# Modulation vectors of a two-layer backbone: silu(c) as the stationary operand in four column tiles

## What is computed

```python
def modulation(cvec, w, b):
    m = jax.nn.silu(cvec) @ w + b
    return [z[:, None, :] for z in jnp.split(m, N_MOD, axis=-1)]

def block(x, mods, nw, fw_in, fw_out, mixer, params, init_state):
    sh1, sc1, g1, sh2, sc2, g2 = mods
    h = rms_norm(x, nw[0]) * (1 + sc1) + sh1
    out, state = mixer(h, init_state, *params)
    x = x + g1 * out
    h = rms_norm(x, nw[1]) * (1 + sc2) + sh2
    x = x + g2 * swiglu(h, fw_in, fw_out)
    return x, state
...
        mods_p = modulation(c_ctx[None, :], mod_w[l], mod_b[l])
        mods_s = modulation(c, mod_w[l], mod_b[l])
```

## Time and profile before

| What | Value |
|---|---|
| Time, median of 3 runs | 3576.94 us (3574.57 to 3578.27) |
| Span of the profiled execution | 3571.6 us |
| TensorE matmul busy | 3069.0 us, 86% of the span |
| TensorE weight loads busy | 2459.5 us, 69% |
| VectorE busy | 1515.4 us, 42% |
| ScalarE busy | 728.8 us, 20% |
| Chain that ended last | TensorE 73%, VectorE 18%, ScalarE 3% |
| Line 377 on that chain | 3% |

### The profile page before, as it was taken

One profiled execution on the slowest core, in us unless ns is written; L12 is line 12 of the kernel. 1 busy time (PEld: TensorE's weight loads), 2 busy tenths in 40 slices (PEclk: granted clock), 3 DMA queues, 4 the chain that ended last, 5 costly groups with the idle time before them and its releaser, 6 DMA issues.

```text
span 3571.6 us, 49794 instructions
## 1 busy us (share of the span) xinstructions
PE 3069.0 (86%) x20104; PEld 2459.5 (69%) x20104; DVE 1515.4 (42%) x2905; ACT 728.8 (20%) x1161; POOL 0.2 (0%) x4
## 2 busy tenths in 40 slices
PE   7799869883999998799989688888887497999897
PEld 6687769763889985588868445555554285888686
DVE  1310655557666562322232336666666513222323
ACT  0321200020111100322221213333333313222211
POOL 0000000000000000000000000000000000000000
PEclk6899556655999977899999889999998698999998
DMA  5122412221000012122212122222222021222121
GB/s 165 41 71 57 118 48 77 75 60 32 5 2 2 2 43 80 42 70 70 70 55 71 37 55 71 72 71 77 73 71 73 7 60 40 71 70 70 56 68 53
DMA packets 404830, 210.10 MB, mean 59 GB/s; under 512 B 13368, under 2 KB 402886, under 8 KB 404550
## 3 DMA queue, kind: packets, MB, share of 16 engines
q1 hardware_dynamic: 345344, 173.36, 16.9%
q10 hardware_dynamic: 59334, 34.66, 3.2%
HBM read 202.32 MB, written 5.67 MB: 58 GB/s over the span
## 4 chain that ended last, share of the span: by engine, by line
PE 73%; DVE 18%; ACT 3%; issue 3%; DVEq 1%; ACTq 1%; DMA 1%
PE bank L250 10%; PE bank L251 9%; PE bank L252 9%; PE bank L253 9%; PE bank L1733 7%; PE bank L377 3%; PE bank L1055 3%; PE bank L230 2%; PE bank L1734 2%; PE bank L443 2%; PE bank L1777 2%; PE bank L1774 2%; PE bank L1107 1%; PE bank L1113 1%; DVE wide_low L270 1%
## 5 line engine op out<-in xcount | busy, mean ns | idle before, releaser
L253 PEld LDWEIGHTS bank<-arena,ring 128*128 128x128 f32 x2816 | 537.3, 191 | 129.0
L253 PE MATMUL bank<-arena,ring 128*128 128x128 f32 x2816 | 545.1, 276 | 0.0
L250 PE MATMUL bank<-h_split,w_split 128*128 128x512 f32 x928 | 450.1, 485 | 65.7 <-DVE w_split L260 65.7
L260 DVE TENSOR_TENSOR w_split<-ring,w_split 128x1024 fp32r<-128x1024 f32 x180 | 214.9, 1201 | 561.3 <-ACT w_split L257 552.4
L1733 PE MATMUL bank<-arena,ring 128*128 128x512 f32 x768 | 410.6, 617 | 2.1 <-ACTq L196 2.1
L251 PE MATMUL bank<-h_split,w_split 128*128 128x512 f32 x928 | 370.2, 399 | 0.0
L252 PE MATMUL bank<-h_split,w_split 128*128 128x512 f32 x928 | 369.3, 398 | 0.0
L257 ACT ACTIVATE w_split<-ring 128x1024 fp32r<-128x1024 f32 x180 | 186.1, 1040 | 729.0 <-PE bank L253 378.4
L250 PE MATMUL bank<-wide_high,w_split 128*128 128x512 f32 x480 | 234.1, 488 | 76.6 <-DVE w_split L260 76.6
L377 PEld LDWEIGHTS bank<-cs_T,ring 128*128 128x128 f32 x1536 | 292.9, 297 | 2.6 <-issue 1.4
L377 PE MATMUL bank<-cs_T,ring 128*128 128x2 f32 x1536 | 288.9, 323 | 2.1 <-ACTq L196 2.1
(11 more groups left out here) (351 smaller groups left out, 4245.2 us busy)
## 6 DMA issues: line engine op xcount, KB each, us to landing
ring<-in_mod_w_dram SPq DMA_DIRECT2D x96, 512.0 KB, 3.7
ring<-in_ffn_w_in_dram SPq DMA_DIRECT2D x88, 512.0 KB, 3.6
ring<-in_od_w_in_dram SPq DMA_DIRECT2D x48, 512.0 KB, 3.8
arena<-cumulative_decays ACTq DMA_DIRECT2D x80, 256.0 KB, 3.5
ring<-in_ffn_w_out_dram SPq DMA_DIRECT2D x32, 512.0 KB, 3.8
ring<-in_ev_w_in_dram SPq DMA_DIRECT2D x30, 512.0 KB, 3.5
ring<-in_od_w_out_dram SPq DMA_DIRECT2D x16, 512.0 KB, 3.8
ring<-in_ffn_w_out_dram SPq DMA_DIRECT2D x16, 384.0 KB, 3.3
```

Of the source, the lines that this page charges most:

```text
L250: E.matmul(o, w_split[:, ws, 0, k, :], high(k), start=st, stop=False)
L253: mm = E.matmul(pair[pr][:, CTX], ring[:, s, k, :], rhs[:, k, CTX], start=st, stop=en)
L260: return V.tensor_tensor(w_split[:, ws, 1, 0:kt], ring[:, s, 0:kt], w_split[:, ws, 0, 0:kt].bitcast(F32), ALU.subtract)
```

## The change

`cs_T` becomes 8 chunks of 32 columns, of which 2 hold data and 30 are zero. It is now the stationary operand, and the weights stream. The class `Mods` works in groups of 8 output tiles (`GT`). A group has two rounds. In a round the four ring slots hold, for 4 of the 8 chunks of features, 256 output columns each: slot s columns 256 s to 256 s + 255. For each chunk, four matmuls write 32 partitions each of one PSUM area of 256 columns, slot s to partitions 32 s to 32 s + 31: four column tiles of TensorE. Over both rounds 32 matmuls accumulate, where there were 64. The last four matmuls of a round count up `unit_done`, so the ring's slots come free at the end of a round. The DMA of a slot takes 4 chunks x 256 columns (runs of 1 KB in memory) instead of 8 x 128 (runs of 512 B), with the same 512 KB.

The result has the two vectors on partitions and outputs along the columns. `copy` (VectorE) brings it to `mod_rows` in SBUF, `turn` (TensorE) transposes its two halves, `bias` (VectorE) adds the bias from PSUM into `mod` and waits for its own end (`mod_made`). Where `stage_mod` and `stage_conv` have two groups, they use two PSUM banks.

The places are these: `stage_mod` two groups; `stage_conv` two groups, all four rounds first and then both turns on TensorE, and on VectorE the copy of group 0 behind the convolutions, the bias of group 0 and the copy of group 1 behind the eighth token shift, the bias of group 1 at the end; the mLSTM head one group, its rounds where units 1, 2 and 3, 4 stood, its turn behind the third chunk of transposes; the mLSTM loop three groups, rounds in iterations 3, 5 and 7 (middle and end), turns in iterations 4, 6 and 8; the other four stages one group each, with rounds in their passes 0 and 1.

Besides, the semaphores of `stage_norm` are shared by all norms, with running counts, the arena is 120 columns smaller, and a memset of `cs_T` stands first on VectorE.

```diff
-    cs_T = sb("cs_T", [P, KD, 2])
+    cs_T = sb("cs_T", [P, KD, 32])
+    mod_rows = sb("mod_rows", [P, 2 * P])
...
+            V.memset(cs_T[:, :, :], 0.0)
...
-    def mod_unit(out, s):
-        for k in range(KD):
-            mm = E.matmul(out, ring[:, s, k, :], cs_T[:, k, :], start=(k == 0), stop=(k == KD - 1))
-        mm.then_inc(unit_done, 1)
...
+        def fetches(self, sp):
+            for g in range(self.ng):
+                t = self.t0 + GT * g
+                w = a["mod_w"][t // 48, :, :].rearrange("(k p) n -> p k n", p=P)
+                for r in range(2):
                     for s in range(4):
+                        c0 = (t % 48) * P + s * 2 * P
+                        sp.wait_ge(unit_done, self.u0 + GT * g + 4 * r + s + 1)
+                        sp.dma_start(ring[:, s, :, :].rearrange("p a b -> p (a b)").rearrange("p (k n) -> p k n", k=4),
+                                     w[:, 4 * r:4 * r + 4, c0:c0 + 2 * P]).then_inc(w_ready[s], 16)
+
+        def products(self, pe, g, r):
+            q = self.u0 // 4 + 2 * g + r
+            for s in range(4):
+                pe.wait_ge(w_ready[s], q * 16 + 16)
+            if r == 0 and g >= len(self.banks):
+                pe.wait_ge(mod_made, self.g0 + g - len(self.banks) + 1)
+            for kk in range(4):
+                k = 4 * r + kk
+                for s in range(4):
+                    w = ring[:, s, :, :].rearrange("p a b -> p (a b)")[:, kk * 2 * P:(kk + 1) * 2 * P]
+                    mm = E.matmul(self.acc(g)[32 * s:32 * s + 32, :], cs_T[:, k, :], w, start=(k == 0), stop=(k == KD - 1))
+                    if kk == 3:
+                        mm.then_inc(unit_done, 1)
+
+        def turn(self, pe, g):
+            pe.wait_ge(mod_copied, self.g0 + g + 1)
+            for h in range(2):
+                mm = E.transpose(self.turned(g)[:, h * P:(h + 1) * P], mod_rows[:, h * P:(h + 1) * P], ident)
+            mm.then_inc(mod_turned, 1)
+
+        def copy(self, dve, g):
+            dve.wait_ge(unit_done, self.u0 + GT * (g + 1) + 4)
+            V.tensor_copy(mod_rows[:, :], self.acc(g)).then_inc(mod_copied, 1)
+
+        def bias(self, dve, g):
+            t = self.t0 + GT * g
+            dve.wait_ge(mod_turned, self.g0 + g + 1)
+            V.tensor_tensor(mod[:, t:t + GT, :].rearrange("p (s h) c -> p s h c", h=2),
+                            self.turned(g).rearrange("p (h s z) -> p s h z", h=2, s=4)[:, :, :, 0:2],
+                            vec[:, V_MODB + t:V_MODB + t + GT].rearrange("p (s h) -> p s h", h=2)
+                            .unsqueeze(3).to_broadcast([P, 4, 2, 2]), ALU.add).then_inc(mod_made, 1)
+            dve.wait_ge(mod_made, self.g0 + g + 1)
...
+            m.copy(dve, 0)
...
+                if k == 7:
+                    m.bias(dve, 0)
+                    m.copy(dve, 1)
+            m.bias(dve, 1)
...
-        return (lambda pe: make(pe, 16)), act, dve, fetches
+        def pe(pe):
+            for g in range(2):
+                for r in range(2):
+                    m.products(pe, g, r)
+            for g in range(2):
+                m.turn(pe, g)
...
-            make_a(pe, 2)
+            ma.products(pe, 0, 0)
...
-            make_a(pe, 2)
+            ma.products(pe, 0, 1)
...
-                make_a(pe, 1 if c < CT else 0)
+                if c == 2:
+                    ma.turn(pe, 0)
...
-                make_b(pe, 1 if n > 2 else 0)
+                if n in (3, 5, 7):
+                    mb.products(pe, (n - 3) // 2, 0)
+                if n in (4, 6, 8):
+                    mb.turn(pe, (n - 4) // 2)
...
-                make_b(pe, 3 if n == 2 else 2 if n > 2 else 0)
+                if n in (3, 5, 7):
+                    mb.products(pe, (n - 3) // 2, 1)
```

More of the change, by code:

```diff
@@ L357, in stage_load @@
         return pe, act, dve
-    MOD0 = 2 * KD
+    GT = 8
     mod_tiles = [0]
[L366 to L371, removed]
-                    for s in range(4):
-                        fetch(sp, s, i + (u0 + a0 - t0) // 4, w[:, :, bass.ds(i * (4 * P) + (a0 - 48 * l + s) * P, P)], KD, P)
@@ L413, in col, with dve @@
+    def stage_mod():
+        m = Mods(2, (4, 5))
+        def pe(pe):
+            m.products(pe, 0, 0)
+            m.products(pe, 0, 1)
+            m.products(pe, 1, 0)
+            m.turn(pe, 0)
+            m.products(pe, 1, 1)
+            m.turn(pe, 1)
+        def dve(dve):
+            for g in range(2):
+                m.copy(dve, g)
+                m.bias(dve, g)
+        return pe, (lambda act: None), dve, m.fetches
     def col(v, n=1):
         return vec[:, v:v + n]
-    def stage_norm(src, dst, kt, scale_at, weight, shift_at, name):
-        sq_s, ss_s, m_s, rt_s, h_s = (sem(f"{name}_{n}") for n in ("squares", "sum", "mean", "root", "scaled"))
+    sq_s, ss_s, m_s, rt_s, h_s = (sem(f"norm_{n}") for n in ("squares", "sum", "mean", "root", "scaled"))
@@ L421, in stage_norm @@
+    norm_tiles, norms = [0], [0]
+    def stage_norm(src, dst, kt, scale_at, weight, shift_at):
+        k0, n0 = norm_tiles[0], norms[0]
+        norm_tiles[0] += kt
+        norms[0] += 1
         sq = dst if kt == KD else take(2, T)
@@ L849, in dve @@
                 dve.sem_inc(st_s, 1)
+                if n in (3, 5, 7):
+                    mb.copy(dve, (n - 3) // 2)
+                if n in (4, 6, 8):
+                    mb.bias(dve, (n - 4) // 2)
                 if n == 1:
@@ L915, in dve @@
                 finish(dve, j)
-            mod_end(dve)
-        return pe, act, dve, fetches
+                if j == 2:
+                    m.copy(dve, 0)
+            m.bias(dve, 0)
+        return pe, act, dve, m.fetches
     def finish_mlstm(ha, vo):
@@ L970, in pe @@
                 mm.then_inc(p_s, 1)
-                make(pe, 2)
+                if j < 2:
+                    m.products(pe, 0, j)
+            m.turn(pe, 0)
         def dve(dve):
```

98 lines of the change are left out of this document (48 added, 50 removed).

## The result

The changed kernel takes 3523.01 us, the kernel before 3575.76: a ratio of 0.9846 (95% interval 0.9832 to 0.986; the quotient of the two medians is 0.9852). The forecast was 25.7 us less, 3551, with a range of 3536 to 3565; the sign was right and the size was not. The profiled execution of the changed kernel takes 3521.53 us, its span is 3519.8 (3571.6 before), so the median lies 3.2 over the span, where the forecast had kept 5.3.

The account below looks back on a forecast made before the run. It took TensorE's 1536 weight loads and matmuls (289 us) as the price, counting where they end a chain of waits. Terms -14.4 +3.2 -13.7 -1.8 +1.5 -0.5 = -25.7: span 3545.9, median 3551 us, range 3536 to 3565.

Parts of the forecast that it names:

- the round (3.6): On TensorE, 16 matmuls of 256 columns in four side-by-side column tiles take 3.6 us at the lower clock.
- the refill in the first stage (8.2): Each later round waits 8.2 us for four 512 KB loads from a standing start; bounds 6.8 and 9.0.
- the head's second round: In the mLSTM head, the second round ends after its refill at 450.3 against 453.02 before: -2.7 us.
- Rivals 1 and 3: Column-tile lanes: 1, overlap only in pairs, round 6.9, total 3607 us, 9%; 3, overlap with loss, round 4.3, 3563, 11%.
- Rival 2: Streaming keeps TensorE's clock at its upper level, so rounds take 1.9 us everywhere: 3539 us; chance 13%.
- Rival 4: Refills are far slower than one transfer suggests, 11 us each, so no change: 3576 us; chance 7%.
- loop iterations of 20 to 21 us throughout: Sign of a right forecast: every mLSTM loop iteration takes 20 to 21 us.
- Place by place: Prediction's sum over the start and the stages with modulation work: -25.7 us from a 3571.6 us span.
- three groups add a copy and a bias, +2.2: In the mLSTM loop, copies and biases with their waits lengthen VectorE's chain by 0.75 us a group.
- the term for the removed units (-4.0): In the mLSTM loop, removing the three units of iteration 2, where TensorE sets the pace, saves 4.0 us.
- The other four groups: Both head norms, RWKV in and out: each adds a VectorE copy, and a refill may end late: +1.5 us.
- the convolution's +3.2: In the convolution, VectorE gets two copies and a bias more, 1.4 us, and waits 1.8 at group 0's bias.

Follow-up runs that it names:

- e2: Changed kernel with the arena 8 words longer, so the split operands lie 32 bytes past a multiple of 64: 3538.26 us, ratio 0.9895.
- e3: Changed kernel with the convolution's group 0 turned ahead of the last round and group 1 copied four steps later: 3523.50 us, ratio 0.9862.
- e6: Changed kernel without the mLSTM loop's three groups, 24 tiles staying zero: loop 197.5 us against 194.9 with them.
- e7: Changed kernel with the first stage's four products of a block in one column tile and four banks: stage 58.8 us against 39.2.
- experiment 4: The run e7: changed kernel, first stage's products in one column tile instead of four; 7.07 us for what four do in 1.94, upper clock level.
- e8: Kernel before with its tiles at the changed kernel's addresses, no instruction different: 3558.97 us, ratio 0.9956.
- experiment 5: The run e6: changed kernel without the mLSTM loop's three groups; loop 197.5 us, against 194.9 with them and 200.3 with the old units.

## Why the prediction missed

**Right.** The bound of each place, the round (3.6), the refill in the first stage (8.2), the order of events in the convolution (bias, turn, queue), the head's second round (-2.6 against -2.7 forecast; in part luck, for in e2, e3, e6 and e7 the first copy behind it comes 1.5 to 1.7 us later), the sign of every place with units but the last group of four. Rivals 1 and 3 fell with the round of 3.4 to 3.64 and with experiment 4. Rival 2 fell in the first stage and the convolution, where seven of eight rounds took 3.4 to 3.64 us; it held in part elsewhere, where nine of sixteen took 1.9 to 3.3. The rule of the Trainium skill ("TensorE: Matmul & The Clock Gate", Part 3, The mechanism), that a weight load overlaps running matmuls only if its row group differs, does not hold for this kernel: four tiles with the same 128 rows run 3.6 times as fast as one, with their loads inside the matmuls' time. The 2.38 that the Trainium skill gives for three column tiles (same page, Part 3, Measured speedup vs the span model) has no run here, but four at 3.6 speak against a loss of that kind. Rival 4 fell: refills of 7.8 to 9.8, not 11. Of the signs named ahead, loop iterations of 20 to 21 us throughout did not come: from the third interval between reciprocals on they take 18.7 to 22.0.

**The step that failed first: "Place by place" summed only the places with units.** It took every other stage as unchanged, since no instruction of theirs is. But the diff shows three sizes (`cs_T`, `mod_rows`, `NAR`) that move every operand behind them, and the earlier trace rows show single instructions of stages without units at most (rows 2, 5 and 10), none of a split product. By e8 this is 16 us (11 to 21); its profiled span shows 13. No row of before could have given sign or size; it belonged into the range as an unknown of its own, and it was not there. With the operands displaced by 32 bytes (e2) the changed kernel takes 3538 us, just inside the range and still 13 from the forecast.

**The second: the clock was one rival of 13% for the rounds alone.** The prediction priced what a faster round would give (rival 2) and left all other work of those stretches at the level that the earlier trace rows show. What those places gave beyond the forecast lies in that other work: the head's transposes and copies at 10.7 us instead of 13.4 (at 1.00 instead of 0.50, VectorE's copies come every 0.72 us, not 0.85 to 1.0), the loop's waits, the head norms and RWKV out. In the loop the term "three groups add a copy and a bias, +2.2" had the wrong sign, by experiment 5 it is -0.6 to -2.7; the term for the removed units (-4.0) measured 0 to -3.4. The other four groups measured -3.4 where +1.5 stood. Together with the head some 12 us. One trace each overstates this a little: over five traces with the old instructions and four with the new ones the mLSTM stage takes 276.7 and 256.5 us on the mean, 20.2 less where the table has 22.3. The clock is shown as the cause for the copies in the head; for the loop it rests on one execution, and for the other four groups on the rows alone (first head norm 0.50 to 0.63, RWKV out 0.68 to 0.73), with no run that tests it. What raised the clock in each place is open.

**The third, against the gain:** the convolution's +3.2 measured +6.0. The refill of 8.2 came from the quietest rows; there it was 9.2 on the mean of three, and all of it lands on the wait. Why two of the three refills were 1.5 us longer was not found; no other queue moved more than one packet of 16 KB.

Of the 26 us or so by which the profiled span lies under the forecast (27 by the medians), 16 are in stages without units: 12 in the three that e8 speeds up by addresses alone, 3.5 in SSD, which varies by that much without a change. Some 12 are in the mLSTM stage and the other four groups, where the clock is the likeliest cause, 1 is in the start, and the convolution takes 3 back.

## What to carry on

When a diff changes the size of a tile, list what is placed behind it, and give the stages that stream from there a range of about 1% either way (the pitch moved by up to 1.4% here). Where the granted clock of a stretch is not at one level, price the work that stays there at both levels, not only the work that is new. And look at when a buffer comes free, not only how often: the same matmuls with a slot freed after four of them instead of sixteen gave another 23 us (e4). With the head's group in the loop it was 28, which the intervals do not tell from e4.

## What the runs showed of the hardware

- Split products stream at 7.31 to 7.41 us a unit by the place of either operand in SBUF, moved in steps of 32 bytes. In six layouts the three with the moving operand on a multiple of 64 bytes are the faster (7.31 to 7.36 against 7.38 to 7.41); the rest of the rule was not found.
- Four column tiles with the same rows and 32 columns each: 1.94 us for 16 matmuls of 256 columns at the upper clock level, 7.07 us in one tile.
- Streams on an engine that waits can cost nothing: with 6 rounds in it the mLSTM loop took 194.7 to 196.9 us in four executions (granted clock 0.69 to 0.72), with none 197.5 in one (0.65).
- A stage with unchanged code and unchanged addresses moved by up to 7 us from run to run (SSD, 726.1 to 733.0, at a granted clock of 0.92 and 0.91), and the head of the mLSTM stage by up to 4 (51.5 to 55.4, 0.70 and 0.66).
